# One transformer block and two mixer layers in fp32 halves on one core: two heads' latent keys in one product, norm rows turned to columns whole, a pair of convolution inputs moved ahead, zeros under the first loads

## The reference

```python
u = _rms_norm(x, mix_norm[l])
c = _split_cols(u @ w_in[l] + b_in[l])
y_sb = _from_heads(_stick_breaking_attention(...))
y_ml = _mlstm(c['ml_q'], c['ml_k'], c['ml_v'], c['ml_o'], c['ml_i'], c['ml_f'],
              ml_conv_w[l], ml_conv_b[l], ml_out_norm[l])
y_mla = _mla(c['mla_cq'], c['mla_ckv'], c['mla_kr'], positions, ...)
g = jax.nn.sigmoid(c['gates'])
merged = g[:, :, 0] * (y_sb @ w_up_sb[l]) + g[:, :, 1] * (y_ml @ w_up_ml[l]) + g[:, :, 2] * (y_mla @ w_up_mla[l])
x = x + merged @ w_out[l]

def _mla(c_q, c_kv, k_rope, positions, q_norm, kv_norm, wq_up, wkv_up, q_gain, k_gain):
    q = (_rms_norm(c_q, q_norm) @ wq_up).reshape(b, s, 4, 96)
    kv = (_rms_norm(c_kv, kv_norm) @ wkv_up).reshape(b, s, 4, 64 + 64)
    k_nope, v = kv[..., :64], kv[..., 64:]
    k = jnp.concatenate([k_nope, k_pe], axis=-1)
    # q and k: rms norm over 96, rope on the last 32, causal softmax attention
```

## Time and profile before

| | us |
|---|---|
| runs | 2364.04, 2365.41, 2365.55 |
| median | 2365.41 |
| profiled execution, from outside | 2363.47 |
| its span | 2361.7 |

### The profile page before, as it was taken

How to read it: one execution, slowest core, us unless ns; L and a number is a source line. 1 busy time by engine, 2 the same in 40 slices (tenths; PEclk the granted TensorE clock), 3 DMA queues, 4 the chain that set the end, 5 groups by cost and what they waited for, 6 DMA issues and landing times.

```text
span 2361.7 us, 29592 instructions
## 1 busy us (share of the span) xinstructions
PE 2340.2 (99%) x11084; PEld 1909.7 (81%) x11084; DVE 1124.1 (48%) x1820; ACT 982.9 (42%) x1561; POOL 1288.7 (55%) x1589
## 2 busy tenths in 40 slices
PE   8999999999999999999999999999999999999999
PEld 8777788888888888777788888888887777888887
DVE  5765375422324432478626733333325785265330
ACT  4566543222223233676534432332336764343321
POOL 5654266655556655456245755555554553466554
PEclk9999999999999999999999999999999999999999
DMA  5322133333333333222122333333332221233333
GB/s 163 100 73 70 55 92 96 99 98 98 96 94 110 99 98 105 72 64 79 54 90 81 99 99 98 97 91 98 98 104 65 71 72 56 88 92 97 97 98 98
DMA packets 60862, 212.88 MB, mean 90 GB/s; under 512 B 6704, under 2 KB 8112, under 8 KB 60720
## 3 DMA queue, kind: packets, MB, share of 16 engines
q1 hardware_dynamic: 60576, 210.86, 29.6%
q10 hardware_dynamic: 144, 0.14, 0.0%
HBM read 208.87 MB, written 2.10 MB: 89 GB/s over the span
## 4 chain that ended last, share of the span: by engine, by line
PE 98%; ACT 1%; DVE 1%; issue 0%; DMA 0%; POOL 0%; SPq 0%; ACTq 0%
PE banks L749 96%; PE banks L1048 0%; PE banks L878 0%; ACT t L1742 0%; PE banks L928 0%; DMA t<-in_xT 0%; DVE t L1251 0%; PE banks L1105 0%; POOL t L2073 0%; DVE t L1440 0%; ACT t L1871 0%; ACT L2034 0%; DVE t L1596 0%; DVE t L1677 0%; DVE t L1478 0%
## 5 line engine op out<-in xcount | busy, mean ns | idle before, releaser
L749 PE MATMUL banks<-t,t 128*128 128x512 f32 (+8 forms) x10796 | 2315.8, 385 | 17.6 <-ACT t L1762 6.3
L749 PEld LDWEIGHTS banks<-t,t 128*128 128x128 f32 (+3 forms) x10796 | 1878.0, 187 | 433.5 <-issue 49.7
L2073 POOL TENSOR_TENSOR t<-t,t 128x256 fp32r<-128x256 f32 x1544 | 1234.4, 830 | 1036.6 <-ACT t L1742 1027.8
L1742 ACT ACTIVATE t<-t 128x1024 fp32r<-128x1024 f32 x385 | 408.2, 1060 | 1087.0 <-issue 584.9
L1251 DVE TENSOR_TENSOR t<-banks,t 128x512 f32<-128x512 f32 x121 | 83.1, 688 | 187.0 <-PE banks L749 186.6
L1421 DVE TENSOR_TENSOR t<-banks,t 128x512 f32<-128x512 f32 x44 | 30.4, 691 | 184.1 <-PE banks L749 184.0
L1389 DVE SCALAR_TENSOR_TENSOR t<-banks,t 128x512 f32<-128x512 f32 x32 | 22.1, 691 | 155.4 <-PE banks L749 155.4
L1134 DVE SCALAR_TENSOR_TENSOR t<-t,t,t 128x512 fp32r<-128x512 f32 x64 | 51.9, 815 | 58.2 <-ACT t L1762 58.1
L1366 DVE TENSOR_TENSOR t<-t,t 128x512 fp32r<-128x512 f32 x68 | 70.1, 1031 | 2.3
L1762 ACT ACTIVATE t<-t,t 128x512 fp32r<-128x512 f32 x64 | 45.5, 715 | 55.6 <-DVE t L1389 48.8
L1395 DVE TENSOR_TENSOR t<-banks,t 128x512 f32<-128x512 f32 x24 | 16.6, 691 | 106.0 <-PE banks L749 106.0
(11 more groups left out here) (190 smaller groups left out, 1224.3 us busy)
## 6 DMA issues: line engine op xcount, KB each, us to landing
t<-in_w SPq DMA_DIRECT2D x386, 512.0 KB, 3.5
t<-in_xT SPq DMA_DIRECT2D x8, 256.0 KB, 6.0
out<-t SPq DMA_DIRECT2D x8, 256.0 KB, 4.6
t<-in_vbias SPq DMA_DIRECT2D x2, 384.0 KB, 3.9
t<-in_c SPq DMA_DIRECT2D x1, 576.0 KB, 9.1
t<-in_w SPq DMA_DIRECT2D x2, 256.0 KB, 4.1
t<-in_pos SPq DMA_DIRECT2D x2, 256.0 KB, 3.7
t<-in_dmask SPq DMA_DIRECT2D x4, 128.0 KB, 4.3
```

The lines of the kernel that those rows point to most:

```text
L749: return pe.matmul(o, l, r, start=start, stop=stop, skip_group_check=True)
L1742: a.activation(whl[u % 2][:, 0:1024], wraw[u % 3][:, :], ACT.Copy).then_inc(*w_high.next(u))
L2073: p.tensor_tensor(hl[:, 1024:2048][:, c], wraw[u % 3][:, c], as_f32(hl[:, c]), ALU.subtract).then_inc(*w_low.next((u, q)))
```

## The change

Four parts.

- **Latent keys.** `kup` has two groups in place of four; a block holds the 64 key columns of two heads, head h in rows 64·(h mod 2) of the bank. DVE still makes one copy for each head, and the bank is freed by the second. Two more pads fill the unit.
- **Third pair.** `ml_proj(3)` goes from behind the mark "mla" to behind `ml_proj(2)`, ahead of the mark "sb" and of all latent groups; the weights' order follows.
- **Columns.** Four whole transposes of 128x128 per set in place of four products of one column, into a bank's full width or, at offset 384, into one quarter each of four banks; DVE copies the first column of each. The strided set of block 1 has its source laid out by an added DVE copy first (`rstd_strided`) and is turned by itself.
- **Zeros.** A step `warm` behind the first loads: DVE sets `rstdB` to zero, PE multiplies it by itself three times (512, 512 and 256 columns, plain fp32) into bank 7. It is entered in the engines' tables of steps too (two hunks of one line, left out below).

```diff
--- before.py
+++ after.py
@@ -114,17 +114,16 @@
         for t in range(2):
             full("cq", "w_in_2", l, K8, W2["cq"] + 128 * t)
         full("ckv", "w_in_2", l, K8, W2["ckv"])
-        for t in range(1, 3):
+        for t in range(1, 4):
             both("mlq", "mlk", t)
-        for h in range(4):
-            put("kup", "mla_wkv_up_2", l, [(0, 128)], [(128 * h, 0, 64)])
+        for t in range(2):
+            put("kup", "mla_wkv_up_2", l, [(0, 128)], [(256 * t, 0, 64), (256 * t + 128, 64, 64)])
         for h in range(4):
             full("qup", "mla_wq_up_2", l, range(2), 96 * h, 96)
         for t in range(2):
             put("vup", "mla_wkv_up_2", l, [(0, 128)], [(256 * t + 64, 0, 64), (256 * t + 192, 64, 64)])
         while len(out) % 8:
             out.append(("pad", None, 0, None, None))
-        both("mlq", "mlk", 3)
         for g in range(MLO_AT):
             full("gt", "w_in_2", l, K8, W2["gate"] + 128 * g)
         for t in range(4):
@@ -340,7 +339,7 @@
 
 
     FIRST = {"norm": "av", "norm_halves": "av", "norm_squares": "av", "head_in": "av", "low_halves": "pav", "conv": "av", "halves1": "av", "half2": "av", "stats": "tav", "stats_beside": "tav",
-             "whalf": "avp", "whalf_rest": "ap", "sb_split": "av", "low_rs": "av"}
+             "warm": "vt", "whalf": "avp", "whalf_rest": "ap", "sb_split": "av", "low_rs": "av"}
 
     def put(self, *step):
         self.steps.append(step)
@@ -614,6 +613,10 @@
 
         def pair(slot):
             return 2 + 2 * slot, 3 + 2 * slot
+
+        def turned(b, o):
+
+            return banks_t[:, 0:4, o:o + 128] if o else B[b].rearrange("p (c n) -> p c n", c=4)
 
 
         posi = reg(60, S, I32)
@@ -817,6 +820,11 @@
                 ins.then_inc(*t_dense.next(("grp", g)))
                 bank[G.bank] = [G.freed]
 
+            def warm():
+                need.wait_ge(*v_norm.at(("warm",)))
+                for n in (512, 512, 256):
+                    mm(B[7][:, 0:n], rstdB[:, 0:128], rstdB[:, 0:n])
+
             def stats(s, b):
                 need.wait_ge(*in_const.at("const"))
                 need.wait_ge(*v_norm.at(("acc", s, 7)))
@@ -838,7 +846,7 @@
                     free(b)
                     bank[b] = [(v_norm, ("cols", name))]
                 for c in range(4):
-                    ins = mm(B[b][:, o + c:o + c + 1], view(src, c), C["ident"][:, 0:1])
+                    ins = pe.transpose(turned(b, o)[:, c, :], view(src, c), C["ident"])
                 ins.then_inc(*t_stat.next(("cols", name)))
 
             def head_sum(hid):
@@ -1120,6 +1128,9 @@
             def norm(s, m):
                 norm_halves(s, m)
                 norm_squares(s, m)
+
+            def warm():
+                v.memset(rstdB, 0.0).then_inc(*v_norm.next(("warm",)))
 
             def half_weights(u):
                 if u in FRONT:
@@ -1178,7 +1189,10 @@
 
             def columns(name, b, o, src, view, dst, tok):
                 need.wait_ge(*t_stat.at(("cols", name)))
-                v.tensor_copy(dst, B[b][:, o:o + 4]).then_inc(*v_norm.next(("cols", name)))
+                v.tensor_copy(dst, turned(b, o)[:, :, 0]).then_inc(*v_norm.next(("cols", name)))
+                if name == ("rc", 1):
+                    v.tensor_copy(sqt.rearrange("p (r n) -> p r n", r=4),
+                                  rstdB.rearrange("p (n r) -> p r n", r=4)).then_inc(*v_norm.next(("rstd_strided",)))
 
             def turns1():
                 need.wait_ge(*in_const.at("const"))
@@ -1555,7 +1569,8 @@
                 need.wait_ge(*t_dense.at(("grp", g)))
                 need.wait_ge(*v_attn.at(("low_kv", l)))
                 reach(need, *sbd)
-                v.tensor_tensor(MK[h][0:64, :], B[groups[g].bank][0:64, :], RKV[0:64, :], M_).then_inc(
+                half = slice(64 * (h % 2), 64 * (h % 2) + 64)
+                v.tensor_tensor(MK[h][0:64, :], B[groups[g].bank][half, :], RKV[half, :], M_).then_inc(
                     *v_evac.next(("kup", l, h)))
 
             def qup(l, h, g, sbd):
@@ -2216,6 +2231,7 @@
 
 
         put("load_cols")
+        put("warm")
         put("load_front")
         put("load_x", 0)
         sch.load(0)
@@ -2248,7 +2264,8 @@
             put("stats_beside", 0, 128)
             yield "t", (v_norm, ("rstd", 0))
             put("cols", ("rc", 1), 0, 384, rstdB, natural, rcol_t[:, 0:4], (v_norm, ("rstd", 0)))
-            put("cols", ("rc", 2), 1, 384, rstdB, strided, rcol_t[:, 4:8], (v_norm, ("rstd", 0)))
+            yield "t", (v_norm, ("rstd_strided",))
+            put("cols", ("rc", 2), 0, 384, sqt, natural, rcol_t[:, 4:8], (v_norm, ("rstd_strided",)))
             yield "v", (t_stat, ("cols", ("rc", 2)))
             put("values1")
             yield "v",
@@ -2618,7 +2635,7 @@
             for t_, (tag, i) in enumerate((("cq", 0), ("cq", 1), ("ckv", 0))):
                 M["cq"].append(proj(tag, s, YL[t_], lay, bcol(l, tag, i)))
             sch.waiting.insert(0, low_item)
-            for t_ in range(1, 3):
+            for t_ in range(1, 4):
                 ml_proj(t_)
             sch.until(("low", l), *[("sb", l, t_) for t_ in range(2)])
             put("mark", ("sb", l))
@@ -2630,8 +2647,8 @@
             ch = [(CHh[i], CHl[i], (v_attn, ("low_half", l, i))) for i in range(3)]
             turn = (v_norm, ("turns2",))
             for h_ in range(4):
-                b = sch.bank()
-                g = sch.dense("kup", b, ch[2:3], freed=(v_evac, ("kup", l, h_)))
+                if h_ % 2 == 0:
+                    g = sch.dense("kup", sch.bank(), ch[2:3], freed=(v_evac, ("kup", l, h_ + 1)))
                 put("kup", l, h_, g, sbd)
                 sch.waiting.append(key_chain(l, h_, R=MK[h_], ones=C["ones"], n=96, tiles=mt, src=[(v_evac, ("kup", l, h_))]))
                 sch.pump()
@@ -2656,8 +2673,6 @@
             sch.skip_pads()
             put("mark", ("mla", l))
             mlr = (("mark", ("mla", l), "tvap"),)
-            ml_proj(3)
-
             def silu_item(slot):
                 yield "a", *[(v_attn, ("conv", l, ch_)) for ch_ in range(8)]
                 put("silus", l)
```

More of the change, by code:

```diff
@@ L1107, in ml_turn @@
                 bank[ba] = [(v_attn, ("ml_open", l, h))]
-            return {"mm": dense, "wide": wide, "small_turn": small_turn, "stats": stats, "stats_beside": stats_beside, "cols": columns, "head_sum": head_sum, "dil_scores": dil_scores, "dil_turn": dil_turn, "dil_values": dil_values,
+            return {"warm": warm, "mm": dense, "wide": wide, "small_turn": small_turn, "stats": stats, "stats_beside": stats_beside, "cols": columns, "head_sum": head_sum, "dil_scores": dil_scores, "dil_turn": dil_turn, "dil_values": dil_values,
                   "swa_scores": swa_scores, "swa_turn": swa_turn, "swa_values": swa_values, "sb_scores": sb_scores,
@@ L1703, in merge2 @@
                 split(MH[m][0], MH[m][1], T[tl[0]], ("mixed", l, m))
-            return {"whalf": half_weights, "norm": norm, "norm_halves": norm_halves, "norm_squares": norm_squares, "stats": stats, "cols": columns, "turns1": turns1, "turns2": turns2,
+            return {"warm": warm, "whalf": half_weights, "norm": norm, "norm_halves": norm_halves, "norm_squares": norm_squares, "stats": stats, "cols": columns, "turns1": turns1, "turns2": turns2,
                     "rope_angles": rope_angles, "values1": values1, "proj": proj, "head_in": head_in, "key_rope": key_rope,
```

## The result

| | before | after |
|---|---|---|
| median, us | 2364.99 (7 runs) | 2371.21 (7 runs) |
| lowest to highest | 2364.04 to 2365.55 | 2369.50 to 2374.07 |
| profiled execution: from outside, span | 2363.47, 2361.7 | 2371.21, 2369.4 |
| mean granted clock, profiled execution | 1.000 | 0.998 |

The ratio is 1.003, its 95% interval 1.002 to 1.0039: slower by some 6 us. The runs spread over 4.6 us where those of before spread over 1.5, and they fall in line with their mean granted clock: 2369.5 and 2369.6 us at 0.999, 2374.07 at 0.996.

The account below looks back on a forecast made before the run. TensorE, busy 2340.2 of 2361.7 us, was taken as the bound. From 2363.47, products and columns took −6.0 and waits added 9.2, giving 2366.7; with 1.94 from that execution to the runs' median, 2368.6 (range 2362.5 to 2374.0).

Parts of the forecast that it names:

- Fewer products, −2.7 us: Latent keys in two layers: 12 products of 0.222 us go from TensorE's chain, −2.7 us.
- the bank that waits for two copies: First query group of each mixer waits for two DVE copies before taking its bank: +0.6 us (0 to 0.7).
- Columns, −3.3 us: Whole transposes for one-column products: 1.8 us less in block 1, 1.5 us less in the mixers; added strided copy hidden.
- Zeros, 0: Program start: faster first products save 2.5 us on TensorE, waited back for weights at 17.58 and 26.09; taken as 0.
- a rival with a chance of 0.05: Clock falls again in longer early waits; 24 products at the low level cost 3.6 us more: 2372.2; chance 0.05.
- The 2.5 us that the prediction estimated by that rule: Rival at the start: activity releases the clock and the end comes 2.5 us earlier, 2366.1; chance 0.05.
- The barrier, +3.4 per mixer: Where the order waits until all eight heads are done: values 1.3, last sum 0.6, next scores 1.5 us (together 0 to 5.6).
- The other small waits, +0.6: Six more DVE taps before the values' and first gate's banks are freed and keys' sums made: +0.6 per mixer (0 to 1.5).
- the cover holds: Rival: DVE's head work is freed of 6.8 us, so the barrier has no wait; 2361.8 or 2359.4 us; chance 0.17.
- 8.2 us of slack, 12.4 taken: Between first key and barrier, per mixer: 12.4 us of TensorE's time go against 8.2 us slack, so 4.2 are missing.
- The whole last head stands open: Rival: next scores need the last head's own banks, waiting 3.7 us in place of 1.5; 2373.0 us; chance 0.18.

Follow-up runs that it names:

- kup_fill: Kernel before plus two-headed keys, whole-transpose columns and two filler products of 384 columns in each mixer's wait before the third latent group; 2363.38 us.
- col_only: Kernel before with only the norm rows turned by whole transposes; 2360.28 us, 0.9981 of the kernel before.
- col_warm: Kernel before with only the whole-transpose columns and the zeros under the first loads; 2360.22 us, ratio 0.9983.
- half_move: Full change, but of the third pair only mlq3 moved ahead of the keys, mlk3 left behind the mark; 2364.07 us, 1.0001 of the kernel before.
- move_only: Kernel before with only the third pair moved ahead of the latent keys; 2379.88 us, ratio 1.0059.
- kup_col: Kernel before with two-headed keys and whole-transpose columns, no zeros, nothing moved; 2364.59 us, ratio 0.9998.
- fill2: Full change plus two filler products before the second scores and two before the third latent group, per mixer; 2367.47 us, 1.0012 of the kernel before.
- warm_only: Kernel before with only the zeros under the first loads; 2364.75 us, ratio 0.9999.

## Why the prediction was partly right

The time, 2371.2, lies in the range (2362.5 to 2374.0), 2.6 us over the forecast. The forecast was a change of +3.2 us, inside the 4.7 us that it took for what can be told from no change, and the result is +6.2, outside them. It was reckoned from a median of 2365.41 in three runs; the seven give 2364.99. By its own steps:

- **Fewer products, −2.7 us.** The products went, the time did not. With the clock kept up, the two-headed keys cost 3.1 us beside the columns, that is 5.8 more than the step says. The prediction had +1.2 of it (the bank that waits for two copies: foreseen 0.6 per mixer, measured 0.97 to 1.70, +0.73). The rest is small waits of 0.2 to 0.5 us in places that it did not look at. The profile of `kup_fill` has the larger of them, in each mixer once. From its table of PE's waits:

```profile
PE banks L1113 <- DVE t L1681: 1.1, 2, 0.5
```

PE's timeline round the latent groups:

```profile
1050.87 7.55 PE L753 MATMUL banks<-t,t 128*128 128x512 f32 x28 [0.31 <-DVE t L1570]
...
1059.30 2.87 PE L753 MATMUL banks<-t,t 128*128 128x128 f32 x24 [0.44 <-POOL t L2085]
```

and later in the same mixer:

```profile
1130.39 1.65 PE L753 MATMUL banks<-t,t 128*128 128x512 f32 x6 [0.40 <-POOL t L2085]
...
1191.62 0.66 PE L1113 MATMUL banks<-t,t 128*128 128x128 f32 x4 [0.53 <-DVE t L1681]
```

- An idle time also understates a wait. The records' ends are modelled: a product stands with 0.396 us, but the next starts 0.222 behind it, so each wait between products of 512 columns costs PE 0.17 us more than its idle time. Ahead of the scores the idle time is 2.72 us, and the 3.85 from the sum's start at 1110.55 to 1114.40 hold two records of one fp32 product, which by the earlier trace rows takes some 0.9: the wait cost 2.9.
- **Columns, −3.3 us.** The size of the direct saving holds: in profiles with the clock at 1.00, `col_only` ends 3.2 us before the kernel before (spans 2358.5 and 2361.7). The medians differ by 4.6, perhaps since the low stretch behind the one-column products went too. The added strided copy was not waited for: no wait on it is in the table of `col_only`.
- **Zeros, 0.** Right, and in the main by the reason given: PE waits back what it gained, but for the second unit at 13.44 us and not at 17.6 and 26.1, where the prediction had put it. In the full change's profile the first 24 real products take 338 ns in the median, and PE then waits 2.29 us until 13.44:

```profile
5.89 5.26 PE L752 MATMUL banks<-t,t 128*128 128x384 f32 x24
13.44 16.93 PE L752 MATMUL banks<-t,t 128*128 128x384 f32 x83 [2.29 <-POOL t L2088]
```

  The windows behind that wait:

```profile
13.90:17.30 3.40, 3.40 (x12) 3.40 (x11) 3.40 (x4) 2.80 (x4) 3.40 (x4) 0.50 0.59 216
17.30:22.00 4.70, 4.70 (x28) 4.70 (x28) 3.12 (x4) 1.62 (x3) 4.27 (x5) 1.00 0.36 119
```

  What was foreseen as a rival with a chance of 0.05 is also there: behind that wait the granted clock is 0.50 from 13.9 to 17.3, in this one of the seven profiles of kernels with zeros. The Trainium skill, page "TensorE: Matmul & The Clock Gate", Part 1, says that the clock is throttled by default and that activity releases it. The trace agrees: with zeros ahead the first real products take 338 ns, where they took 522. The 2.5 us that the prediction estimated by that rule are given back: `col_warm` is no faster than `col_only`.
- **The barrier, +3.4 per mixer.** PE's idle time is 0.58 + 2.72 = 3.30 in mixer 0, 0.58 + 2.73 in mixer 1. The sum is luck, since its parts were sized less well and their errors cancel: the values did not wait at all (1.3 foreseen; the cast came behind ACT's copies, not ahead of them), the last sum waited 0.58 (0.6), the scores 2.72 (1.5, bounds 0 to 3.1), because another head's two passes stood ahead of the last query's four operations.
- **The other small waits, +0.6.** Mixer 1, which ran at 1.00 there, took 3.12 us longer; the prediction's terms for a mixer, 4.6 − 1.3 (keys) − 0.4 (one set of columns), make 2.9. Here too errors cancel. The prediction had −2.7 + 1.2 = −1.5 us for the keys, measured +3.1, and for the moved pair 2 × (3.4 + 0.6) = 8.0, measured 4.1.
- **The step that failed** is the one that is not in the sum: the clock behind the barrier. The prediction let it fall only at the start, and called that unlikely. It reckoned waits as if PE went on at full speed behind them. In the profile that cost 2.3 us in mixer 0; over the runs, filling the two waits of each mixer takes away 3.7 us and leaves 2367.5, 1.1 under the forecast of 2368.6. So the waits were nearly right in sum, by luck, and the clock took the time to the upper part of the range. A second step that failed is the price of the keys, as said above.
- Of the rivals, "the cover holds" failed as reckoned (8.2 us of slack, 12.4 taken), and `half_move` showed its other side: with 7.0 taken it does hold. "The whole last head stands open" did not come: the scores did not wait for that head's own banks.

## What to carry to other kernels

Read from the schedule how many microseconds of independent work lie between the start of a slow chain and the point that waits for it, and what slack the last link has; a change that took less than the slack was free (`half_move`), one that took more was not, and the count did not say how much it would pay (`move_only`). Where PE is busy 99% of the span, removing products can lose time: here six fewer in a mixer came with more waits than they had cost. Look also at the order on the engine that is waited for: here VectorE stood idle for 2.17 us and then did 5 us of other work ahead of the small copy that freed the bank. And price a wait of one or more microseconds on TensorE with the low clock that may follow it: here that came to 3.7 us, half of the 7.2 that keys and moved pair cost without it, and it differs from run to run, so one profile may not show it.

## What the runs showed of the hardware

- The granted clock fell behind waits of PE as short as 1.7 us: in `kup_col` 0.50 from 1051.0 to 1054.2, behind the wait for the third latent group.

```profile
1051.00:1054.20 3.20, 3.20 (x8) 1.92 (x6) 1.96 (x3) 3.10 (x5) 0.00 (x0) 0.50 0.62 164
1054.20:1060.00 5.80, 5.70 (x25) 4.07 (x23) 2.57 (x5) 4.42 (x8) 0.70 (x2) 1.00 0.00 0
```

  It did not fall each time: the same two waits left it at 1.00 in mixer 1 of the full change and took it to 0.50 in mixer 0. With two products of no use in the wait it was 1.00 at that place in both mixers of the profile, and the mean clock was 1.000 in ten of eleven runs where both waits were filled (`fill2`), against none of the seven of the full change.
- Busy on record is not enough to keep it: behind a stretch of eight products with a single column each, in which PE counted as busy throughout (2.66 of 2.66 us in the kernel before), it fell in two of the four profiles of kernels that have them (`warm_only` from 45.3 us, `move_only` from 43.6).
- The spread between runs goes with such falls. The eleven runs of `col_only`, all at 1.000, lie within 1.2 us; the runs of the kernel before, at 0.999 to 1.000, spread over 4.1 to 4.7 us in the three sets of 27.
